# Two decoder layers on one core: attention steps regrouped by head, copies and splits reordered around the norms, table loads requested elsewhere

## The reference

```python
# layer 0: gated short convolution beside attention, one input and one output projection
h, gb, gc, q, k, v = split(rms_norm(x) @ w_in)
ya = gb * causal_dwconv(gc * h)
yb = window_attention(q, k, v)       # 8 query heads of 64, 2 kv heads, window 128, ALiBi, sinks
x = x + rms_norm(concat(ya, yb) @ w_out)
x = x + rms_norm(conv_ffn(rms_norm(x)))
# layer 1: HGRN2, a gated linear recurrence, 8 heads of 128
q, f, i, g = split(rms_norm(x) @ w_in_c)
o = recurrence(q, 1 - lb, f, i)      # lb: lower bounds from a softmax over two rows of logits
x = x + rms_norm((rms_norm(o) * silu(g)) @ w_out_c)
x = x + rms_norm(conv_ffn(rms_norm(x)))
```

## Time and profile before

| | |
|---|---|
| three executions | 1425.98, 1426.84, 1426.47 us; median 1426.47 |
| profiled execution | 1428.36 us, of which the span of the trace is 1426.6 |
| granted clock of TensorE, mean | 0.98 of full speed |
| busy | PE 1380.8 us (97%), DVE 831.1 (58%), ACT 589.0 (41%), POOL 246.9 (17%) |

### The profile page before, as it was taken

One profiled execution on the slowest core, in us unless ns is written; L12 is line 12 of the kernel. 1 busy time (PEld: TensorE's weight loads), 2 busy tenths in 40 slices (PEclk: granted clock), 3 DMA queues, 4 the chain that ended last, 5 costly groups with the idle time before them and its releaser, 6 DMA issues.

```text
span 1426.6 us, 27953 instructions
## 1 busy us (share of the span) xinstructions
PE 1380.8 (97%) x10672; PEld 1342.9 (94%) x10672; DVE 831.1 (58%) x1401; ACT 589.0 (41%) x1174; POOL 246.9 (17%) x373
## 2 busy tenths in 40 slices
PE   9999999999999999996999999989999999999997
PEld 8988898999999999986999999989899999999996
DVE  6457566655666522266677777766766555563224
ACT  5344445433333322255565555545533333332221
POOL 2123220111111100002222222221121111111000
PEclk9989999999999999998999999999999999999998
DMA  7311230322222322212222222214022222233211
GB/s 273 108 45 45 62 117 30 102 84 84 85 88 87 122 82 98 68 45 87 92 90 75 90 75 88 84 53 136 30 75 88 88 88 88 88 116 107 89 41 63
DMA packets 39680, 123.34 MB, mean 86 GB/s; under 512 B 4232, under 2 KB 12040, under 8 KB 39496
## 3 DMA queue, kind: packets, MB, share of 16 engines
q1 hardware_dynamic: 35400, 111.92, 24.8%
q10 hardware_dynamic: 4048, 10.20, 1.9%
q0 software_dynamic: 176, 0.44, 0.1%
HBM read 113.98 MB, written 8.57 MB: 86 GB/s over the span
## 4 chain that ended last, share of the span: by engine, by line
PE 84%; DVE 10%; issue 3%; ACT 2%; DMA 1%; ACTq 0%; POOL 0%; SPq 0%; DVEq 0%; POOLq 0%
PE acc L428 73%; PE aux L704 3%; DVE w_lo L1281 2%; DVE x L1483 1%; PE aux L746 1%; PE aux L583 1%; DVE mix L1478 1%; PE aux L603 1%; DVE lev L1634 1%; DVE h_lo L1290 1%; DVE scratch L1736 1%; PE aux L718 1%; DVE lev L1628 1%; PE aux L740 1%; PE aux L595 0%
## 5 line engine op out<-in xcount | busy, mean ns | idle before, releaser
L1281 DVE TENSOR_TENSOR w_lo<-raw,w_hi 128x512 fp32r<-128x512 f32 (+1 forms) x372 | 317.2, 855 | 369.7 <-ACT w_hi L827 369.1
L428 PE MATMUL acc<-h_hi,w_hi 128*128 128x272 f32 x2208 | 480.9, 296 | 11.6 <-DVE scratch L1319 5.0
L428 PE MATMUL acc<-h_hi,w_lo 128*128 128x272 f32 x2208 | 468.9, 291 | 0.0
L428 PE MATMUL acc<-h_lo,w_hi 128*128 128x272 f32 x2208 | 468.1, 290 | 0.0
L428 PEld LDWEIGHTS acc<-h_hi,w_hi 128*128 128x128 f32 x2208 | 354.4, 191 | 23.2 <-issue 6.6
L827 ACT CAST w_hi<-raw 128x512 fp32r<-128x512 f32 (+1 forms) x372 | 236.4, 642 | 319.2 <-PE acc L428 314.4
L428 PEld LDWEIGHTS acc<-h_lo,w_hi 128*128 128x128 f32 x2208 | 354.9, 191 | 0.2
L428 PEld LDWEIGHTS acc<-h_hi,w_lo 128*128 128x128 f32 x2208 | 352.1, 191 | 0.0
L428 PE MATMUL acc<-g_hi,w_hi 128*128 128x272 f32 x704 | 153.2, 289 | 0.0
L428 PE MATMUL acc<-g_hi,w_lo 128*128 128x272 f32 x704 | 153.2, 289 | 0.0
L428 PE MATMUL acc<-g_lo,w_hi 128*128 128x272 f32 x704 | 152.6, 288 | 0.0
(11 more groups left out here) (244 smaller groups left out, 1517.6 us busy)
## 6 DMA issues: line engine op xcount, KB each, us to landing
raw<-in_w_up SPq DMA_DIRECT2D x88, 512.0 KB, 3.5
raw<-in_w_down SPq DMA_DIRECT2D x32, 704.0 KB, 4.0
raw<-in_w_in_c SPq DMA_DIRECT2D x32, 512.0 KB, 3.5
raw<-in_w_in_ab SPq DMA_DIRECT2D x18, 512.0 KB, 3.7
raw<-in_w_out_ab SPq DMA_DIRECT2D x8, 512.0 KB, 3.6
S<-in_state ACTq DMA_DIRECT2D x8, 512.0 KB, 4.0
o_ss<-Snew ACTq DMA_DIRECT2D x8, 512.0 KB, 2.7
raw<-in_w_out_c SPq DMA_DIRECT2D x8, 512.0 KB, 3.5
```

The lines of the kernel that those rows point to most:

```text
L428: mm = pe.matmul(acc[out][:, t, 0:H], w[slot][:, wc], mv[:, kk_, t * H:(t + 1) * H], start=start and k == 0 and q == 0, stop=stop and k == ...
L1281: dve.tensor_tensor(w_lo[slot][:, to], raw[n % 4][:, cols], w_hi[slot][:, to], ALU.subtract).then_inc(lo_ready, 1)
```

## The change

- **Attention steps.** Step s serves query block n = s // 2 and a pair of heads of each kv group. The four score matmuls alternate between partitions 0 to 63 and 64 to 127 and between banks A[0] and A[1]. The output is made of four matmuls of 256 columns (two in steps 0 and 1) that alternate between the lower and upper 64 partitions of A[2]. Bias columns and sinks are permuted to match (on the host for the sinks). y_hi and y_lo are formed from 128 partitions by 256 elements, where it was 64 by 512.
- **After output products.** VectorE copies tile 5 out inside its loop of the norm's first part, then tiles 6 and 7, and does all four splits behind them. ScalarE does its copies for these splits inside its own loop. Slots 8 and 4 change places between units 2 and 3 of the FFN, so the wait for the slot moves to unit 3. TensorE's wait ahead of the first pair stays only for the recurrence's phase.
- **After the first FFN.** The last tile's second part is copied out after tile 4 of the norm, not after tile 6.
- **Recurrence.** Tables and state are requested inside ScalarE's loop over the tiles of t=1; VectorE waits for them ahead of the first scan. Both parts of the lower bounds, and ScalarE's Exp between them, move to the start of the norm after the first output product.

```diff
@@ slot_of, and slot_free of ScalarE
-            return (4, 8)[n - UNIT0[name] - 2]
+            return (8, 4)[n - UNIT0[name] - 2]
...
                     if u == 2:
-                        act.wait_ge(half_done, 2 * (UNIT0[out] + 4) + h_ + 1)
                         return
                     if u == 3:
+                        act.wait_ge(half_done, 2 * (UNIT0[out] + 4) + h_ + 1)
                         return
@@ TensorE
-                pe.wait_ge(evac, TILE0[name] - 1)
+                if pre == 2:
+                    pe.wait_ge(evac, TILE0[name] - 1)
...
-                for j in range(GRP):
-                    mm = pe.matmul(A[j // 2][:, (j % 2) * 256 + lo_k:(j % 2) * 256 + 256],
-                                   q_sb[rows, j, n * WIN:(n + 1) * WIN],
-                                   k_sb[rows, (n - 1) * WIN + lo_k:(n + 1) * WIN], start=True, stop=True)
+                for j in range(2):
+                    for g in range(2):
+                        rows = slice(64 * g, 64 * g + 64)
+                        mm = pe.matmul(A[g][:, j * 256 + lo_k:j * 256 + 256],
+                                       q_sb[rows, 2 * pair + j, n * WIN:(n + 1) * WIN],
+                                       k_sb[rows, (n - 1) * WIN + lo_k:(n + 1) * WIN], start=True, stop=True)
...
                 for c in range(first, 2):
-                    mm = pe.matmul(A[2][64 * g:64 * g + 64, :], vtok[:, n - 1 + c, 64 * g:64 * g + 64], pT[:, c, :],
-                                   start=c == first, stop=c == 1)
+                    for g in range(2):
+                        rows = slice(64 * g, 64 * g + 64)
+                        mm = pe.matmul(A[2][rows, 0:256], vtok[:, n - 1 + c, rows], pT[:, c, 256 * g:256 * g + 256],
+                                       start=c == first, stop=c == 1)
@@ ScalarE, attention_hi (VectorE's attention_lo alike)
-                act.copy(y_hi[r, 0:GRP, n * WIN:(n + 1) * WIN], A[2][r, :].rearrange("p (j q) -> p j q", j=GRP)
-                         ).then_inc(yb_hi, 1)
+                act.copy(y_hi[:, 2 * pair:2 * pair + 2, n * WIN:(n + 1) * WIN],
+                         A[2][:, 0:256].rearrange("p (j q) -> p j q", j=2)).then_inc(yb_hi, 1)
@@ ScalarE, after_out
+                if post == 1:
+                    act.wait_ge(C["lb_ready"], 1)
+                    act.activation(lb[:, 1:3, :], lb[:, 1:3, :], ACT.Exp).then_inc(C["lb_done"], 1)
                 norm_root(post, S[3], 0)
                 for k in range(KD):
                     normed_tile(pre, 0, k, gain)
                     normed_square(0, k)
-                    if k in (0, 3, 5):
-                        out_square(out, post, {0: 2, 3: 3, 5: 4}[k], 1)
-                split(m + 4, 0)
-                out_square(out, post, 5, 1)
-                split(m + 5, 0)
-                split(m + 6, 0)
+                    if k in (0, 3, 5, 7):
+                        out_square(out, post, {0: 2, 3: 3, 5: 4, 7: 5}[k], 1)
+                    if k in (2, 4, 6, 7):
+                        split(m + {2: 4, 4: 5, 6: 6, 7: 7}[k], 0)
                 out_square(out, post, 6, 1)
-                split(m + 7, 0)
                 out_square(out, post, 7, 1)
@@ ScalarE, after_down
-                    if k == 5:
+                    if k == 4:
                         last_out(post, 1)
                         split(m + 3, 0)
...
+                    if k < 4:
+                        to, table = ((keep, "c_keep"), (masks, "c_masks"), (mask_s, "c_mask_s"), (own, "c_own"))[k]
+                        act.dma_start(to[:], dram[table]).then_inc(const_c, 16)
+                    if k == 5:
+                        act.dma_start(S0[:], dram["state0"][0, :, :, :]).then_inc(state0_in, 16)
                 norm_root(2 * pre, rstd, 0)
@@ VectorE, after_out
+                if post == 1:
+                    lower_bounds_a()
+                    lower_bounds_b()
...
-                        if t == 0 and k in (0, 3, 5):
-                            out_cols(out, pre, {0: 2, 3: 3, 5: 4}[k], 1)
+                        if t == 0 and k in (0, 3, 5, 7):
+                            out_cols(out, pre, {0: 2, 3: 3, 5: 4, 7: 5}[k], 1)
                     if t == 0:
-                        split(m + 4, 0)
-                        out_cols(out, pre, 5, 1)
-                        split(m + 5, 0)
-                        split(m + 6, 0)
                         out_cols(out, pre, 6, 1)
-                        split(m + 7, 0)
                         out_cols(out, pre, 7, 1)
+                        for q in range(4, 8):
+                            split(m + q, 0)
@@ VectorE, after_down
-                        if t == 0 and k == 6:
+                        if t == 0 and k == 4:
                             last_out(u_done, pre, 1)
@@ VectorE, hgrn_tick of head 0 (gone from ahead of head(0))
+                    if prev is None:
+                        dve.wait_ge(const_c, 64)
+                        dve.wait_ge(set_up, 5)
                     dve.wait_ge(C["lf_ready"], cur + 1)
```

More of the change, by code:

```diff
@@ L576, in scores @@
             def scores(s):
-                n, g = divmod(s, 2)
+                n, pair = divmod(s, 2)
                 lo_k = WIN if n == 0 else 0
-                rows = slice(64 * g, 64 * g + 64)
                 pe.wait_ge(s_biased, 2 * s + 2)
-                for j in range(GRP):
-                    mm = pe.matmul(A[j // 2][:, (j % 2) * 256 + lo_k:(j % 2) * 256 + 256],
-                                   q_sb[rows, j, n * WIN:(n + 1) * WIN],
-                                   k_sb[rows, (n - 1) * WIN + lo_k:(n + 1) * WIN], start=True, stop=True)
+                for j in range(2):
[4 more added lines that the diff above has]
+                                       k_sb[rows, (n - 1) * WIN + lo_k:(n + 1) * WIN], start=True, stop=True)
                 mm.then_inc(s_done, 1)
@@ L598, in attention_out @@
             def attention_out(s):
-                n, g = divmod(s, 2)
+                n = s // 2
                 pe.wait_ge(pT_copied, 2 * s + 4)
@@ L932, in attention_hi @@
                     return
-                n, g = divmod(s, 2)
-                r = slice(64 * g, 64 * g + 64)
-                act.copy(y_hi[r, 0:GRP, n * WIN:(n + 1) * WIN], A[2][r, :].rearrange("p (j q) -> p j q", j=GRP)
-                         ).then_inc(yb_hi, 1)
+                n, pair = divmod(s, 2)
+                act.copy(y_hi[:, 2 * pair:2 * pair + 2, n * WIN:(n + 1) * WIN],
+                         A[2][:, 0:256].rearrange("p (j q) -> p j q", j=2)).then_inc(yb_hi, 1)
             extra = {12: [lambda: vT(0), lambda: vT(1)], 13: [lambda: vT(2), lambda: exps(-1)],
@@ L1144, in _ @@
             ffn(0)
-            act.wait_ge(C["lb_ready"], 1)
-            act.activation(lb[:, 1:3, :], lb[:, 1:3, :], ACT.Exp).then_inc(C["lb_done"], 1)
             STEPS_C = 7
@@ L1360, in softmax_in @@
                 else:
-                    g = s % 2
+                    pair = s % 2
                     w = slice(WIN, 2 * WIN) if s < 2 else slice(0, 2 * WIN)
@@ L1365, in softmax_in @@
                     for a in range(2):
-                        dve.tensor_tensor(pr[g][:, 2 * a:2 * a + 2, w],
+                        dve.tensor_tensor(pr[pair][:, 2 * a:2 * a + 2, w],
                                           A[a][:].rearrange("p (j k) -> p j k", j=2)[:, :, w],
-                                          bias[:, 4 * g + 2 * a:4 * g + 2 * a + 2, w], ALU.add).then_inc(s_biased, 1)
-                    view, sink = pr[g][:, :, w], vec[:, V_SINK + 4 * g:V_SINK + 4 * g + 4]
-                    z = sm[:, g]
+                                          bias[:, 4 * a + 2 * pair:4 * a + 2 * pair + 2, w], ALU.add
+                                          ).then_inc(s_biased, 1)
+                    view, sink = pr[pair][:, :, w], vec[:, V_SINK + 4 * pair:V_SINK + 4 * pair + 4]
+                    z = sm[:, pair]
                 dve.wait_ge(s_biased, 2 * s + 4)
@@ L1396, in attention_lo @@
                     return
[L1397 to L1400, removed]
+                n, pair = divmod(s, 2)
+                j, c = slice(2 * pair, 2 * pair + 2), slice(n * WIN, (n + 1) * WIN)
+                dve.tensor_tensor(y_lo[:, j, c], A[2][:, 0:256].rearrange("p (j q) -> p j q", j=2),
+                                  y_hi[:, j, c], ALU.subtract).then_inc(yb_lo, 1)
             extra = {12: [lambda: softmax_in(-1)], 13: [lambda: softmax_sum(-1)], 16: [lambda: attention_lo(-1)]}
@@ L1801, in head @@
                     hgrn_tick(t, prev, hd)
[L1803 to L1806, removed]
             head(0, None, 0)
@@ L2009, in _layouts @@
         + [cols(f["hgrn_lb_logits"][l]) for l in range(2)] + [cols(f["hgrn_norm_g"][0])]
-        + [np.broadcast_to(sinks, (P, 8)), sinks[4 * (row // 16 % 2) + row // 4 % 4][:, None]], 1)
+        + [np.broadcast_to(sinks.reshape(2, 2, 2).transpose(1, 0, 2).reshape(8), (P, 8)), sinks[4 * (row // 16 % 2) + row // 4 % 4][:, None]], 1)
```

4 lines of the change are left out of this document (removed).

## The result

The changed kernel takes 1405.0 us (median of 4 runs, 1403.33 to 1406.02), the kernel before 1426.65 on the same chip (1425.98 to 1427.19). The ratio is 0.9847, with a 95% interval of 0.983 to 0.9864: 21.65 us faster, where 19.7 were forecast.

A forecast was written before the change was run, and what follows sets the result against it. TensorE, busy for 97% of the span, was taken to bound the kernel. Attention 7.6, norms after output products 5.0 and the norm ahead of the recurrence 7.1 sum to 19.7 us: median 1406.8, range 1400.5 to 1413.

The forecast's parts named there:

- half of the old time plus 0.13: Attention score and output matmuls: estimated new time of each group with two array halves at once; 11.8 us shorter together.
- that rival: Attention scores: two row halves don't run at once, scores give 0, total gain 16.5 us, 1410.0 us; chance 0.15.
- The reason given, alternation: Attention matmuls: neighbours alternate between array halves and so run at once; 6.3 us from scores, 5.5 from outputs.
- The rule that spoke against it: Attention outputs: column halves share rows, so each pass would show its weight load and outputs give clearly less than 5.5 us.
- the squares' row: Profile row for the sums of squares: 8 matmuls on four 32-column parts take 1.05 us, so all parts run at once.
- Conv again, its maximum 0.9 late because of that little slack: Attention stage, sixth of seven periods, with a convolution: VectorE 10.75 us against TensorE 9.25, a stall of 1.5 us.
- the light period: Attention stage, fifth period: VectorE takes 8.7 us, so no stall, with 0.55 us of slack left.
- VectorE keeps up: Attention stage: no new stalls, all 11.8 us gained, total 23.9, 1402.6 us; chance 0.13.
- 1.0 + 5.0 + 1.4 - 0.3: Norm ahead of the recurrence: earlier copy 1.0, no table wait 5.0, full clock 1.4, less requests in ScalarE's loop 0.3.
- The rival that requests hold ScalarE: Recurrence's tables: requests hold ScalarE or tables land no sooner, so this part gives 3 us, 1410.9 us; chance 0.08.
- In the old places they lay under waits: nothing back: Lower bounds' little operations ahead of the recurrence: moving them away gains 0 us there.
- The slower rival: Attention stage: packed passes and new stalls drop the clock to half, some +45 less 19.7, about 1452 us; chance 0.04.

The follow-up runs named there:

- the run of this part alone: The kernel before with only the change's attention part, norms, tables and lower bounds as before: 1417.01 us, ratio 0.9934.
- the ordered groups: Two kernels, each the changed kernel with the four score or the four output matmuls of a step ordered group by group: 1405.1 and 1405.05 us.
- the convolution early: The changed kernel with VectorE's convolution moved to ahead of the softmax sum of the step before: 1400.85 us, ratio 0.9819.
- requests only: The changed kernel with the wait for the tables back ahead of the first head's copies, requests still in the norm's loop: 1403.08 us, ratio 0.9838.
- requests late: The changed kernel with the five table requests back behind the norm's root, the wait left at the scan: 1406.1 us, ratio 0.9854.
- y_lo first: The changed kernel with VectorE's subtraction for y_lo ahead of the weight split and the convolution in each even step: 1402.43 us, ratio 0.9821.

## Why the prediction was right

It said 1406.8 and 1405.0 was measured, inside the range. The mechanisms that carry the sum held: halves at once, stalls behind y_lo, earlier copies, no wait for a table and full clock behind it. What it got wrong is in the terms.

- **Attention matmuls.** Forecast 11.8 shorter. From the chain: scores 0.43 + 1.05 + 6 x 0.86 = 6.6, outputs 2 x 0.42 + 6 x 0.85 = 5.9, together 12.5. (With one block of keys the old outputs took 1.00, not the 0.93 that the forecast halved.) Right; the "half of the old time plus 0.13" was 0.02 to 0.05 too much at full clock. The second score step took 0.95 for 1.13 forecast; in the run of this part alone, where it lies wholly at half clock, it took 1.15. Two row halves do run at once, which no row of before showed, so that rival is out. The reason given, alternation, was wrong: the ordered groups are as fast.
- **The rule that spoke against it.** Eight output passes on two column halves take 1.01 or 1.02 us, alternating or in order, and their weight loads of 136 ns each lie inside running passes. The Trainium skill, "TensorE: Matmul & The Clock Gate", Part 3, in its list of what overlaps, lets a weight load overlap only where the row group differs; by that rule the outputs would have kept much of their 1.86. The traces disagree, as the squares' row had said.
- **Stalls.** Forecast 0, 0, 0.8, 0.85, 0, 1.5, 1.8; measured 0, 0, 0.83, 0.77, 0, 0.82, 1.83. All in their places, one mis-sized: "Conv again, its maximum 0.9 late because of that little slack". From the transposes at 123.61 to the end of y_lo at 133.49 it was 9.88 us, not 10.75, the same as in the first period with a convolution (94.48 to 104.36): the light period before it had given all of the lateness back. There the slack was misread: y_lo ended at 121.01, 2.6 us ahead of the transposes (GpSimd's normalisation at 122.4, 1.2 ahead), where 0.55 was counted, since w_lo took 0.69 (119.98) and not the 2.38 and 2.39 of the periods before and after it; why is open. The zero of that period came out all the same. 3.4 us net (4.25 less 0.89) in place of 4.2. The rival "VectorE keeps up" is out; one line, the convolution early, makes it come true but for 0.9 us.
- **Attention in all.** Forecast 7.6 net; 12.5 less 3.4 is 9.1. The part alone measured 9.1 by the medians; its trace has 10.0 from the first scores to the statistics, 1.1 of them the clock's (a half-clock stretch of 6.8 us for 10.2). The profiled run has 11.3: 2.3 more come from the clock at the sample step, whose output matmuls (6.67 us down to 5.18) and next half (5.23 down to 4.41) ran longer at 2.4 GHz. The forecast allowed 1.5 either way for this. In the traces of the kernels with the old attention the half-clock stretch there is 10.2, 6.8 and 10.2 us long, in those with the new one 3.4 or 6.8: shorter in the mean, but not a fixed size. Two kernels with one and the same attention stage have 3.4 (requests only) and 6.8 (requests late), so a part of this execution's 2.3 is luck.
- **The two norms after output products.** Forecast 2.5 each, measured 2.5 each, in the changed kernel and alone. The step by step timing held.
- **The norm ahead of the recurrence.** Forecast 7.1: 1.0 + 5.0 + 1.4 - 0.3. Measured 7.4: 1.1 by the sums of squares, and 6.3 for the wait and the clock, which were put at 6.4; the 0.3 of requests is nothing. The rival that requests hold ScalarE is out. The step "In the old places they lay under waits: nothing back" doesn't hold for the second part of the lower bounds: with the wait for the table gone they would have been the next thing to hold the copies, until 648.2. The sum came out because the same change moved them.
- **The slower rival.** No half clock shows between 81 and 155 in any trace of the new attention. Stalls of up to 1.8 us didn't bring it.

In sum 19.7 were forecast for the profiled execution and 24.2 came: 3.7 of the difference in the attention stage (0.7 matmuls, 0.8 stalls, 2.3 clock, less 0.1 lost ahead of it), 0.3 at the tables, 0.4 in the heads; the last 0.1 is rounding. By the medians it is 19.7 against 21.65. The medians lie nearer than the profiled executions, since the one of before lies 1.7 us above its median and that of after 0.85 below.

## What to carry to other kernels

When a change makes the bound engine faster, time the second engine's loop from one release to the next, stage by stage: the forecast of stalls made this way from the old trace held to 0.1 us in six of seven periods, once with the wrong slack behind it. The same timeline shows where the next edit belongs: in the idle time ahead of a result that the second engine waits for. Where two edits are aimed at one wait, try each alone, since here either removed all of it, and look on the timeline for what would hold the engine next: here it was the lower bounds, which only a third edit took away. A gain of a few microseconds at a place near a clock drop should be read from the events around it, and not from the end of the span, which moved by up to 7.2 us between runs of one kernel (y_lo first).

## What the runs showed that had not been expected

- Matmuls on different halves of the array run at once in both orders tried: 1.07 us for eight passes in order against 1.06 alternating, where eight passes on one half took 1.92.
- A DMA request in ScalarE's program starts beside an operation and costs nothing where the engine has 0.33 us of idle time a tile.
- 38 matmuls that nobody reads, 8.5 us of them in two gaps of 4.3 and 2.5 us, held the clock at 2.4 GHz and gave 1.0 us by the first outer product, although they outlasted the gaps.
- One kernel's times go with its mean granted clock: 1395.4 us at 0.993, 1400.05 at 0.990. The 0.003 between them is about 4.2 us of 1400 (an estimate), most of the 4.7 that lie between the times.
